# Joining the gated delta rule's front and the state-space angles to the two attentions, with a shorter routing and joined ends, in a two-block transformer kernel on one core

## What is computed

```python
# first block, gated delta rule: the "front" makes q, k, v rows, beta, g and the norms
q = l2norm(heads(q)); k = l2norm(heads(k)); v = heads(v)
beta = sigmoid(b_logit)
g = -exp(a_log) * softplus(a_logit + dt_bias)      # then a cumulative sum per chunk of 64
# second block, state space: the angles and tables of the recurrence
dt = exp(log_dt); mag = exp(lr * dt)
ab_re, ab_im = mag * cos(li * dt), mag * sin(li * dt)
...
# mixture of experts: routing, then the experts, then the end
g_p, g_idx = top_k(softmax(xt @ w_group + b_group), 1)
e_p, e_idx = top_k(softmax(chosen group's logits), 2)
w = g_p * e_p / sum(e_p)
...
x = x + g2 * hier_moe(h, ...)
return rms_norm(x, final_g)
```

## Time and profile before

| what | us |
|---|---|
| median of 3 runs (lowest, highest) | 1857.25 (1855.82, 1861.77) |
| the profiled execution, its own time | 1857.5 |
| its span in the trace | 1856.2 |
| before PE's first matrix instruction | 17.7 |
| fence before the dilated attention, fence behind it | 184.4, 229.9 |
| last factor of the delta rule's front | 251.7 |
| compression stage, from the last narrow columns | 975 to 1036.2 |
| sparse attention with the state space | 1036.2 to 1256 |
| routing, to the first transpose of gathered rows | 1485.3 to 1523.7 |
| experts | 1523.7 to 1820.5 |
| end | 1820.5 to 1856.2 |

### The profile page before, as it was taken

One profiled execution on the slowest core, in us unless ns is written; L12 is line 12 of the kernel. 1 busy time (PEld: TensorE's weight loads), 2 busy tenths in 40 slices (PEclk: granted clock), 3 DMA queues, 4 the chain that ended last, 5 costly groups with the idle time before them and its releaser, 6 DMA issues. The chain is left out here.

```text
span 1856.2 us, 23943 instructions
## 1 busy us (share of the span) xinstructions
PE 1680.1 (91%) x9050; PEld 1260.8 (68%) x9050; DVE 941.0 (51%) x1851; ACT 720.5 (39%) x1604; POOL 244.6 (13%) x225
## 2 busy tenths in 40 slices
PE   6999969978999999979998699999999939999991
PEld 4887759967888888867877477877888823333330
DVE  4752464545666676664427766643336661222215
ACT  3432762235333334453323566664334521212211
POOL 0000016001222220000000011110010112333320
PEclk9999979989999999989999799999999959999996
DMA  6321000042344442422300000006222348999953
GB/s 255 116 91 46 1 1 1 1 182 90 152 186 185 185 182 96 183 91 105 123 0 24 4 5 8 8 8 249 91 91 91 137 180 350 401 374 387 391 201 152
DMA packets 40080, 251.66 MB, mean 136 GB/s; under 512 B 17760, under 2 KB 17888, under 8 KB 23456
## 3 DMA queue, kind: packets, MB, share of 16 engines
q1 hardware_dynamic: 23120, 223.49, 30.8%
q10 hardware_dynamic: 3024, 15.07, 2.1%
q0 software_dynamic: 13824, 11.58, 1.9%
HBM read 293.99 MB, written 18.87 MB: 169 GB/s over the span
## 5 line engine op out<-in xcount | busy, mean ns | idle before, releaser
L600 ACT ACTIVATE units<-arena 128x512 fp32r<-128x512 f32 (+1 forms) x434 | 261.2, 626 | 487.2 <-PE banks L2206 483.1
L1185 DVE TENSOR_TENSOR units<-arena,units 128x512 fp32r<-128x512 f32 x388 | 263.8, 704 | 290.6 <-ACT units L600 290.3
L2204 PE MATMUL banks<-hx,units 128*128 128x512 f32 x800 | 315.2, 394 | 2.8 <-DVE arena L1633 1.7
L2205 PE MATMUL banks<-hx,units 128*128 128x512 f32 x800 | 312.3, 390 | 0.0
L2206 PE MATMUL banks<-hx,units 128*128 128x512 f32 x800 | 312.3, 390 | 0.0
L600 ACT ACTIVATE arena<-banks 128x512 f32<-128x512 f32 (+3 forms) x238 | 135.0, 571 | 267.9 <-PE banks L2141 101.8
L2141 PE MATMUL banks<-arena 128*128 128x128 f32 (+3 forms) x700 | 116.6, 301 | 67.3 <-ACT arena L600 17.7
L2204 PEld LDWEIGHTS banks<-hx,units 128*128 128x128 f32 x800 | 151.0, 189 | 34.4 <-issue 3.4
L2206 PEld LDWEIGHTS banks<-hx,units 128*128 128x128 f32 x800 | 150.8, 189 | 31.8
L2205 PEld LDWEIGHTS banks<-hx,units 128*128 128x128 f32 x800 | 151.0, 189 | 30.8
L2204 PE MATMUL banks<-units 128*128 128x512 f32 x416 | 164.3, 395 | 6.1 <-DVE units L1185 6.0
(11 more groups left out here) (409 smaller groups left out, 2411.9 us busy)
## 6 DMA issues: line engine op xcount, KB each, us to landing
arena<-in_moe_gu SPq DMA_DIRECT2D x32, 2048.0 KB
arena<-in_w_in SPq DMA_DIRECT2D x17, 2048.0 KB
arena<-in_moe_dn SPq DMA_DIRECT2D x32, 1024.0 KB, 9.1
arena<-in_ada SPq DMA_DIRECT2D x12, 2048.0 KB
arena<-in_w_gu SPq DMA_DIRECT2D x11, 2048.0 KB
arena<-in_w_out SPq DMA_DIRECT2D x4, 2048.0 KB
arena<-in_w_down SPq DMA_DIRECT2D x4, 2048.0 KB
arena<-in_cmp_w SPq DMA_DIRECT2D x2, 2048.0 KB
```

Source lines behind the costliest of these rows:

```text
L600: return func(dst, src, ACT.Copy, scale=scale)
L1185: tt(U[:, u % 4, 1, :], src, U[:, u % 4, 0, :].bitcast(F32), SUB).then_inc(*up("gemm_dve", "lo", c.part, u))
L2204: pe.matmul(bs[i], sh[:, q], mh, start=c.first and k == 0, stop=False)
L2205: pe.matmul(bs[i], sh[:, q], ml, start=False, stop=False)
```

## The change

1. **Start.** ACT loads the first 80 columns of the parameters at once, behind the first constants, and waits for these alone; the other 1291 columns are loaded behind the first chunk. SP waits for `w_in0` to land before it asks for `w_in1`.
2. **Front of the delta rule.** It becomes a second generator `gdn_front()` on PE, DVE and ACT beside the dilated attention. `GDN_TURN` gives one of the 12 groups of transposes to every third step from 8 on. The attention keeps 3, 2 and 2 banks, the eighth goes to the front. The squares move from ACT (32 instructions with a sum) to DVE (one product and one sum for each of 8 groups). The factors of the first two tiles are made there too; the other two and POOL's four stay behind the fence.
3. **State space.** Rotations 1 to 3, the tables and the sines leave the compression stage and stand in the first 12 steps (`LEAD`) of `ssm()`, which then has 124 steps. Three small tables move to the room of constants.
4. **Routing.** Fewer and wider DVE operations; the wait for the exponentials stands behind `mks`; the counting has 3 products instead of 28; PE starts the table of tokens after half of `ohi`; the numbers of the experts (`idh`) are made before DVE waits for that table.
5. **Ends.** DVE takes both halves of `rows_out` and multiplies by the gain `g2` there. The end has two DVE operations per tile instead of three, the table for the root is loaded early, `x4[0]` is multiplied by the last gain before the root is known, and ACT makes the first of the four last products.

```diff
+    a.dma_start(m.col[:, 0:80], I["cols"][:, 0:80]).then_inc(*up("dma_ln", by=16))
-        if t == 0:
-            a.dma_start(m.col, I["cols"]).then_inc(*up("dma_col", by=16))
-    a.wait_ge(*at("dma_col"))
+    a.wait_ge(*at("dma_ln"))
+    a.dma_start(m.col[:, 80:], I["cols"][:, 80:]).then_inc(*up("dma_col", by=16))
...
+        if name == "w_in0":
+            sp.wait_ge(*at("ring0", "w_in0"))
...
+LEAD = 12
+
+GDN_TURN = {8 + 3 * i: divmod(i, 3) for i in range(12)}
...
+    def gdn_front():
+        ch = Chain(a, s, "gdn_act")
+        a.wait_ge(*at("gdn_dve", "absx"))
+        func(G3(0), lb[:, :, 0:4], ACT.Exp, scale=-1.0).then_inc(*up("gdn_act", "expb"))
+        ch(func(G3(11), G3(11), ACT.Exp, scale=-1.0))
+        func(m.al, C["alog"], ACT.Exp).then_inc(*up("gdn_act", "alog"))
+        func(G3(11), G3(11), ACT.Ln, bias=1.0).then_inc(*up("gdn_act", "softplus"))
+        for i in range(43):
+            yield
...
+            t, n = GDN_TURN.get(i - 1, (0, 0))
+            if n == 2:
+                for h in range(4):
+                    copy(m.Vb[:, t, H4[h]], s.bank("gdn", "qkv", t, 2)[:, H4[h]],
+                         g[:, 0, 4 * t + h:4 * t + h + 1]).then_inc(*up("gdn_act", "qkv", t, 2))
+            if i == 41:
+                root("gqk", m.g[:, 6:8, :].rearrange("p a b -> p (a b)"), m.rs_tmp[:, 0:32])
...
+            t, n = GDN_TURN.get(i - 1, (0, 2))
+            if n < 2:
+                b = s.bank("gdn", "qkv", t, n)
+                v.wait_ge(*at("gdn_pe", "qkv", t, n))
+                rows = (m.qt, m.kt)[n][:, t, :]
+                ch(v.tensor_copy(rows, b), "qkv", t, n)
+                ch(tt(m.gjunk[n], rows, rows, MUL))
+                v.reduce_sum(g[:, 6 + n, 4 * t:4 * t + 4], hv(m.gjunk[n]), AX).then_inc(*up("gdn_dve", "sums", t, n))
...
-    run(attention("swa", swa_pairs, 1, m.swa_P, m.swa_T, m.yb, (0, 1, 2, 3), (4, 5), (6, 7)))
+    run(attention("swa", swa_pairs, 1, m.swa_P, m.swa_T, m.yb, (0, 1, 2), (3, 4), (5, 6)), gdn_front())
...
     def ssm():
+        for i in range(LEAD):
+            yield
+            if i == 7:
+                ssm_turns()
...
+        for f in range(1, 4):
+            yield
+            yield
+            ssm_rot(f)
+        yield from ssm_tables()
...
-        copy(m.yo[n % 4][:, 0:512], s.bank("moe", key, i, 0)).then_inc(*up("moe_act", "yo", n))
...
-        v.tensor_copy(m.yo[n % 4][:, 512:1024], s.bank("moe", key, i, 1)).then_inc(*up("moe_dve", "yo", n))
+        for half in range(2):
+            q = slice(512 * half, 512 * half + 512)
+            v.wait_ge(*at("moe_pe", key, i, half))
+            if n >= 4 and half == 0:
+                v.wait_ge(*at(f"yo{n % 4}", n - 4))
+            tt(m.yo[n % 4][:, q], s.bank("moe", key, i, half), m.grow[:, q], MUL).then_inc(*up("moe_dve", "yo", n, half))
...
-        ch(stt(y1, y1, R(5)[:, t:t + 1], m.grow, MUL, MUL))
-        ch(tt(m.x4[:, t, :], m.x4[:, t, :], y1, ADD), "x", t)
+        ch(stt(m.x4[:, t, :], y1, R(5)[:, t:t + 1], m.x4[:, t, :], MUL, ADD), "x", t)
...
-    for t in range(4):
-        group(b[:, 32 * t:32 * t + 32], [(K["triS"], m.mks[:, t, :])] + [(ones, m.mks[:, u, :]) for u in range(t)])
-    group(b[:, 128:160], [(ones, m.mks[:, t, :]) for t in range(4)]).then_inc(*up("route_pe", "pos"))
+    pe.matmul(b[:, 0:128], K["triS"], m.mks[:, 0, :], start=True, stop=False)
+    pe.wait_ge(*at("route", "sums", 3))
+    pe.matmul(b[:, 32:128].rearrange("p (t n) -> p t n", t=3), ones, m.mks[:, 0:3, 0:32], start=False, stop=False)
+    pe.matmul(b[:, 128:160], ones, m.mks[:, 3, 0:32], start=False, stop=True).then_inc(*up("route_pe", "pos"))
```

More of the change, by code:

```diff
@@ L849, in act_program @@
     fence(0)
-    run(attention("swa", 4, 1, m.swa_P, m.swa_T, m.swa_st, m.yT[:, 4:8, :]))
-    fence(1)
     g = m.g
     G3 = lambda i: g[:, i, :].rearrange("p (t h) -> p t h", t=4)
-    lb = m.lgt.rearrange("p (t c) -> p t c", t=4)
-    ch = Chain(a, s, "gdn_act")
-    def squares(t):
-        for i in range(2):
-            a.wait_ge(*at("gdn_dve", "qkv", t, i))
-            for h in range(4):
-                func(m.gjunk[8 * t + 4 * i + h], (m.qt, m.kt)[i][:, t, H4[h]], ACT.Square,
-                     accum_out=g[:, 6 + i, 4 * t + h:4 * t + h + 1]).then_inc(*up("gdn_act", "sq", t, i, h))
-        a.wait_ge(*at("gdn_pe", "qkv", t, 2))
-        a.wait_ge(*at("gdn_dve", "beta"))
-        for h in range(4):
-            copy(m.Vb[:, t, H4[h]], s.bank("gdn", "qkv", t, 2)[:, H4[h]],
-                 g[:, 0, 4 * t + h:4 * t + h + 1]).then_inc(*up("gdn_act", "qkv", t, 2))
@@ L884, in act_program @@
+    run(attention("swa", 4, 1, m.swa_P, m.swa_T, m.swa_st, m.yT[:, 4:8, :]), gdn_front())
+    fence(1)
     for t in range(4):
@@ L1494, in dve_program @@
     fence(0)
-    run(attention("swa", 4, lambda i: table_of(2 * (i // 8) + i % 2), m.swa_P, m.swa_st, swa_finish))
-    fence(1)
     g = m.g
-    ch = Chain(v, s, "gdn_dve")
     G3 = lambda i: g[:, i, :].rearrange("p (t h) -> p t h", t=4)
-    lb = m.lgt.rearrange("p (t c) -> p t c", t=4)
-    def rows_of(t):
-        for i, dst in enumerate((m.qt, m.kt)):
-            v.wait_ge(*at("gdn_pe", "qkv", t, i))
-            v.tensor_copy(dst[:, t, :], s.bank("gdn", "qkv", t, i)).then_inc(*up("gdn_dve", "qkv", t, i))
@@ L1543, in dve_program, with factors @@
+    def factors(t):
         for n, (src, fi) in enumerate(((m.kt, 7), (m.kt, 8), (m.qt, 6))):
@@ L1546, in dve_program @@
             tt(m.gtmp[(4 * t + n) % 8], hv(src[:, t, :]), fac(fi, t), MUL).then_inc(*up("gdn_dve", "op", t, n))
+    fac = lambda i, t: bc(g[:, i, 4 * t:4 * t + 4].unsqueeze(2), 4, 128)
+    run(attention("swa", 4, lambda i: table_of(2 * (i // 8) + i % 2), m.swa_P, m.swa_st, swa_finish), gdn_front())
+    fence(1)
+    ch = Chain(v, s, "gdn_dve")
+    factors(2)
+    factors(3)
     def rows_R(t):
@@ L1914, in dve_route @@
     ch(tt(R(4), R(3), R(2), SUB), "esub")
+    mk2, mks, q_, bp = m.mk2, m.mks, m.q_, m.bp
+    nov, cum, ob, hk = m.nov, m.cum, m.ob, m.hk
+    blk, pos = bp[:, 0], bp[:, 1]
+    bk, ik = m.bi[:, 0:8].rearrange("p (k t) -> p k t", k=2), m.bi[:, 8:16].rearrange("p (k t) -> p k t", k=2)
+    for k in range(2):
+        ch(tt(mk2[:, k].rearrange("p t (g e) -> p t g e", g=4), bc(go.unsqueeze(3), 4, 4, 8),
+              bc(oh[k].unsqueeze(2), 4, 4, 8), MUL))
+    ch(tt(mks[:, 0, :], fl2(mk2[:, 0]), fl2(mk2[:, 1]), ADD), "mks")
+    for t in range(1, 4):
+        ch(tt(mks[:, t, 0:32], mks[:, t - 1, 0:32], mks[:, 0, 32 * t:32 * t + 32], ADD), "sums", t)
+    v.wait_ge(*at("route_act", "gexp"))
+    ch(v.reduce_sum(R(1), ge, AX))
+    ch(v.reciprocal(R(1), R(1)))
     v.wait_ge(*at("route_act", "eexp"))
@@ L2275, in bank @@
             return take(("ssm", *key), until, among=(7,))
+        for _ in range(LEAD):
+            yield
         for f in range(4):
```

304 lines of the change are left out of this document (147 added, 157 removed).

## The result

| | before | after |
|---|---|---|
| median (lowest to highest), us | 1859.08 (1855.82 to 1861.77), 4 runs | 1826.85 (1825.30 to 1831.12), 4 runs |
| span of the profiled execution | 1856.2 | 1824.0 |

A forecast was written before the change was run, and what follows sets the result against it. PE was taken to be at work in all long stages, so gains come only where it idles. Terms of −4.6, −7.5, −2.3, −10.5, 0 and −7.4 sum to −32.3, from 1857.5 to 1825 us; range 1812 to 1842.

The forecast's parts named there:

- Start: Kernel start: ACT no longer waits for the DMA of `cols`; 4.6 us faster, bounds 3 to 5.
- Front of the delta rule: Front joined to the dilated attention, to the end of ACT's factor copies: 7.5 us faster; between 14.4 faster and 5.6 slower.
- E: Dilated attention: how much later its last division ends because of the joined front work; 9.4 us, bounds 2.8 to 22.8.
- Compression and sparse attention: Compression 14.3 us shorter, sparse attention +12.0 (first 12 units 23.7): 2.3 faster; bounds 6 faster to 11 slower.
- Routing: First maximum to `idx`: fewer DVE operations and counting products, though `idx` stands behind `idh`; 10.5 us faster, bounds 8 to 13.
- Experts: Experts stage: DVE takes over the left half of 24 evictions under cover of its waits for PE; 0 us.
- End: Kernel end: `g2` operations, root's table load and part of the last products leave the path; 7.4 us faster, bounds 5 to 8.5.
- Between the stages: Delta rule to compression stage, and sparse attention to routing's first maximum: no change forecast, 0 us for each row.
- The sign of an end of 28: Kernel end: sign that would show the forecast true, an end of 28 us in place of 35.7.
- the turns don't add up: Rival, dilated attention: each DVE turn delays a minimum by 2.16 us, E 22.8 instead of 9.4, total 1838; chance 0.13.
- the lead's loads: Sparse attention's first steps: ACT's sines and table loads, 6.3 us, pass hidden; rival that they add up, 1838, chance 0.10.
- the evictions are off the path: Experts: the opposed rival had DVE's evictions come on the path, costing 50 us, total 1875; chance 0.03.

The follow-up runs named there:

- experiment 2: Changed kernel plus 14 unread PE transposes in its 2.55 us wait for the dilated attention's first exponential: 1826.1 us.
- experiment 9: Changed kernel plus unread transposes in twelve long waits of PE, 8 to 66 at each: 1820.4 us, ratio to before 0.9788.
- experiment 1: Changed kernel with the front's logarithm on ScalarE replaced by an exponential, so one table load and not three precedes the attention's first exponential: 1827.1 us.
- experiment 4: Kernel before the change, with 3 banks of scores instead of 4 in the dilated attention and nothing else: 1861.9 us, ratio 1.0014.
- experiment 5: Changed kernel with every transpose of the front's turns made twice, 96 instead of 48: 1832.5 us.
- experiment 3: Changed kernel with the front's logarithm and the chain of decays 12 to 14 steps later in the dilated attention: 1830.7 us, ratio to before 0.9844.
- experiment 8: Changed kernel with the four operations giving `idx` put ahead of the second half of the operations on `idh`: 1825.7 us.
- experiment 11: Changed kernel with the experts' evictions again shared by ScalarE and VectorE without `g2`, and the `g2` multiplication back in the end: 1835.3 us.
- experiment 10: Changed kernel with the changes of experiment 7, experiment 8 and experiment 9 together: 1811.2 us, ratio to before 0.9735.
- experiment 12: The kernel of experiment 10 with VectorE taking each turn of the front one attention step later: 1811.5 us.
- experiment 7: Changed kernel with one of the three moved rotations back in the compression stage and 10 instead of 12 steps of lead: 1824.2 us.

## Why the prediction was right, and where only in sum

- **Start** (4.6, measured 4.0). Right in mechanism; the first chunk gives back 0.6. The first scores came between 179.9 and 181.3 in all kernels with this start.
- **Front of the delta rule** (7.5, measured 3.2; 5.1 to 5.9 in the three other profiles of the same code). The step that failed is the sum for E: it has terms for ACT, PE and DVE, and none for the attention's own products at half clock. It took the clock of the stage before (0.98) for the joined stage. This profile lost 3.0 to a low stretch at its beginning (experiment 2), the others 1.1 to 1.8. The transposes for which I reckoned with that clock did meet it: only the first of the twelve groups stands in the stretch. At full clock 1.2 more than forecast remain (E = 10.6 against 9.4), and the tail is 0.5 longer. With the clock kept, in experiment 9, the term is −7.9.
- The parts of E at full clock (experiment 2): ahead of the first turn 4.1 against 2.8 for ACT. ACT's part there is 3.0 (PE's first transposes 5.98 behind its scores instead of 2.97), of which the two loads are 2.3 (experiment 1). I had nothing for the missing bank, which costs 0.8 in experiment 4. From the first turn on it is 6.5 against 6.6, but that hit is in part luck: by experiment 5 the 48 transposes account for 4.0, and the other 2.5 are left for DVE's and ACT's part in the turns, which I had put at nothing. (0.66 against 0.98 makes 5.2 of the 7.7, not the 5.3 that the sum has.)
- The Trainium skill (ScalarE: Activation LUTs, "What ACT_TABLE_LOAD costs") counts 2.66 us for a switch. In this trace the loads are 1.28 and the next operation starts within 0.02 behind; two loads fewer brought PE's first transposes 2.3 earlier and made the stage 1.9 shorter, and not the 5.3 of two such switches. The trace decides against the page's figure here.
- **Compression and sparse attention** (2.3, measured 4.2). 14.7 and 23.3 against 14.3 and 23.7. The balance at the far end, +10.5 instead of +12.0, is the size that was off. But the same code varied: experiments 1, 3, 8 and 11, with a low stretch from 1002 to 1006 on, give 284.6 to 284.8 for this row of the table, which is a term of only −1.7 to −1.8. So the forecast lies within what the runs gave, and the excess of 1.9 isn't a finding. That one of three rotations had been free is shown; I didn't draw the consequence that it should stay.
- **Routing** (10.5, measured 10.7). Each of its three times hit within 0.2. (The operations listed for `idh` add up to 6.1 and not to the 5.6 that the sum has; measured are 5.7.) That `idx` loses by standing behind `idh` was forecast at 2 and measured at 2.6 (experiment 8), of which 1.5 reached the first transposes.
- **Experts** (0, measured −2.7). Not the evictions (experiment 11). Kernels with the new routing gave 292.8 to 295.1, and 291.0 to 291.5 with `idx` first; the two with the old gave 296.1 and 296.4. PE's waits for `moe_gu` were 7.2 in all before and 5.7 after. What in the routing makes that difference stays open.
- **End** (7.4, measured 6.3). The x stage gives 5.1, root 1.0, last products 1.2. Then 1.0 comes back: from DVE's last operation (1819.34) to the end of the span it is 4.6, before 3.6 (1852.60 to 1856.2). The sign of an end of 28 didn't come true. ACT and DVE finish two tiles at one moment, and the four stores (issued one every 1.3 us before) come closer together. That the stores are the new bound was not tested.
- **Between the stages** (0, measured −1.2). The row to the compression stage is 712.0 to 712.8 in the kernels with the change (but for those of experiments 9, 10 and 12) and 713.8 and 714.7 in the two without; the row to the routing varies from 222.1 to 224.7 with the low stretches behind the sparse attention. What makes the first difference wasn't traced.

So the total agreed because 6.0 us too much in three terms (start, front, end) met 6.0 too little in the others. That is luck: the mechanisms held, but the sizes of the front and the experts didn't. The rivals: the turns don't add up at 2.16 (E is 10.5 at full clock, not 22.8), though at 3.6 most of the added length shows; the lead's loads were hidden as forecast; the evictions are off the path.

## What to carry to other kernels

Moving work beside a stage on PE is priced with the clock that the stage will have, not the one it had: look at every gap that the change leaves or makes in PE's list, above all at a stage's start. Filling such gaps with transposes that nobody reads took 6 to 8 us off a kernel that seemed full, and a result hidden behind another engine's wait (`idx` behind `idh`, a rotation out of a free place) is found by comparing when each side is ready. A profile's total can agree for wrong reasons, so cut both spans at the same instructions before judging a term, and cut several profiles of the same code before calling 1 or 2 us an effect.

## What the runs showed of the hardware

- PE's granted clock fell to half in or right behind long gaps of PE (at 242, 368, 430, 816, 1242 and 1478 in the changed kernel, in gaps of 7.0, 5.4, 6.4, 10.2, 2.8 and 5.1 us) and came back some us after work resumed. A gap of 2.5 us at 1002.6 left it full in this profile; in five others (experiments 1, 3, 7, 8 and 11) it fell right behind it. In the dilated attention it fell at 184.0, behind gaps of only 0.9, 0.4, 0.8 and 0.6 us. Fourteen transposes in the 2.55 us that follow kept it full in experiments 2, 9 and 10; in experiment 12, with the same transposes, it was low from 183.2 to 186.6.
- The same code doesn't meet the same low stretches. In the dilated attention's beginning the low stretch is 10.2 us long in the changed kernel and 3.4 in experiment 8, whose code is the same up to the routing: the stage is 43.88 and 41.92. Where it lies counts too: 10.2 us from 3.6 behind the first scores cost 3.0, and from 0.7 or 1.0 behind them (experiments 7 and 11) 1.8. Behind the sparse attention it is 6.8, 10.2 or 13.6, and the first 300 products take from 68.1 to 70.6. An early gain of 2 or 3 us can vanish in this way later, as in experiments 1 and 2, so a term should be read at its own place. The Trainium skill (TensorE: Matmul & The Clock Gate, "Part 1: The HAM clock gate") says that where the clock comes up varies from run to run with its phase, and puts the penalty of that ramp under 1% of a typical kernel's span. The first is so here, by the stretches of 3.4 and 10.2 us on the same code. On the second, 8.2 of 1824 us, 0.4%, came back with twelve filled waits, so several such ramps together stay under the page's 1%.
